# Streaming encoder step: norms transposed by token tile, first FFN products among the transpositions, wide sums handed over by tile

## What is computed

```python
xn = rmsnorm(x, g_mix);  proj = xn @ w_in            # first norm, then 9728 columns
h  = x + (gate_a * y_a + gate_b * y_b) @ w_out       # D x D
hn = rmsnorm(h, g_ffn)                               # second norm
gate, up = split(hn @ w_ffn_in)                      # 2 x 5632 columns
gate_c = causal_conv3(gate) + conv_b
h  = h + (silu(gate_c) * up) @ w_ffn_down            # 5632 x D
y  = rmsnorm(h, g_final)
```

## Time and profile before

| | |
|---|---|
| runs | 2498.18 us, median of 3 (2497.25 to 2504.71) |
| profiled execution | 2497.85 us by the same clock as the runs, span 2496.2 us |
| busy share of the span | PE 97 %, PEld 89 %, DVE 44 %, ACT 35 %, POOL 4 % |
| PE waits over 1 us | 15.9 us at the start for parameters, 7.9 us before the second norm's transpositions, some shorter |
| mean granted clock of PE | 0.989 of full |

### The profile page before, as it was taken

How to read it: one execution, slowest core, us unless ns; L and a number is a source line. 1 busy time by engine, 2 the same in 40 slices (tenths; PEclk the granted TensorE clock), 3 DMA queues, 4 the chain that set the end, 5 groups by cost and what they waited for, 6 DMA issues and landing times.

```text
span 2496.2 us, 44147 instructions
## 1 busy us (share of the span) xinstructions
PE 2431.5 (97%) x17372; PEld 2232.2 (89%) x17372; DVE 1104.6 (44%) x1743; ACT 870.8 (35%) x1311; POOL 108.6 (4%) x182
## 2 busy tenths in 40 slices
PE   6999999999899999999998999999999999999997
PEld 6888888888899999999877999999878999999886
DVE  4555656654433322344333544444233444444234
ACT  4444344443323322344223433333222333333232
POOL 4000000000010100000000000000000000000010
PEclk9999999999999999999999999999999999999999
DMA  5323222222533433344533344444333444444433
GB/s 167 105 74 81 78 77 74 74 72 71 132 119 94 124 98 92 96 127 125 169 124 109 112 126 126 126 126 124 127 126 118 132 126 126 126 127 141 128 129 127
DMA packets 414538, 284.14 MB, mean 114 GB/s; under 512 B 31728, under 2 KB 392690, under 8 KB 413536
## 3 DMA queue, kind: packets, MB, share of 16 engines
q1 hardware_dynamic: 405600, 259.16, 35.3%
q0 software_dynamic: 8832, 23.36, 3.4%
HBM read 275.55 MB, written 6.92 MB: 113 GB/s over the span
## 4 chain that ended last, share of the span: by engine, by line
PE 95%; DVE 2%; ACT 1%; DMA 1%; issue 1%; POOL 0%; DVEq 0%; SPq 0%; POOLq 0%; ACTq 0%
PE banks L1453 20%; PE banks L903 19%; PE banks L907 18%; PE banks L904 18%; PE banks L324 2%; PE banks L916 2%; PE banks L918 2%; PE banks L917 2%; PE banks L392 1%; PE banks L1316 1%; PE banks L472 1%; PE banks L1319 1%; PE banks L457 1%; PE banks L1414 1%; PE banks L485 0%
## 5 line engine op out<-in xcount | busy, mean ns | idle before, releaser
L893 DVE TENSOR_TENSOR w_lo<-w_raw,w_hi 128x1024 fp32r<-128x1024 f32 x482 | 590.1, 1225 | 964.5 <-ACT w_hi L888 964.2
L903 PE MATMUL banks<-x_hi,w_hi 128*128 128x384 f32 x2640 | 918.6, 348 | 8.3 <-DVE w_lo L893 8.3
L907 PE MATMUL banks<-x_hi,w_lo 128*128 128x384 f32 x2640 | 886.9, 336 | 0.0
L904 PE MATMUL banks<-x_lo,w_hi 128*128 128x384 f32 x2640 | 885.7, 335 | 0.0
L888 ACT ACTIVATE w_hi<-w_raw 128x1024 fp32r<-128x1024 f32 x482 | 511.3, 1061 | 1039.9 <-PE banks L907 595.5
L903 PEld LDWEIGHTS banks<-x_hi,w_hi 128*128 128x128 f32 x2640 | 497.6, 188 | 35.6 <-issue 11.9
L904 PEld LDWEIGHTS banks<-x_lo,w_hi 128*128 128x128 f32 x2640 | 498.5, 189 | 5.0 <-issue 0.3
L907 PEld LDWEIGHTS banks<-x_hi,w_lo 128*128 128x128 f32 x2640 | 497.6, 188 | 1.2 <-issue 1.2
L1453 PE MATMUL banks<-w_hi,act_hi 128*128 128x512 f32 x528 | 164.2, 392 | 4.6 <-DVE h_rows L2009 2.4
L1453 PE MATMUL banks<-w_lo,act_hi 128*128 128x512 f32 x528 | 164.2, 392 | 0.0
L1453 PE MATMUL banks<-w_hi,act_lo 128*128 128x512 f32 x528 | 163.2, 390 | 0.0
(11 more groups left out here) (401 smaller groups left out, 2294.4 us busy)
## 6 DMA issues: line engine op xcount, KB each, us to landing
w_raw<-in_w_ffn_in SPq DMA_DIRECT2D x176, 512.0 KB, 4.0
w_raw<-in_w_in SPq DMA_DIRECT2D x144, 512.0 KB, 3.8
w_raw<-in_w_ffn_down SPq DMA_DIRECT2D x88, 512.0 KB, 3.6
w_raw<-in_w_out SPq DMA_DIRECT2D x32, 512.0 KB, 3.6
w_raw<-in_w_o_a SPq DMA_DIRECT2D x16, 512.0 KB, 4.0
w_raw<-in_w_o_b SPq DMA_DIRECT2D x16, 512.0 KB, 3.9
w_raw<-in_w_in SPq DMA_DIRECT2D x20, 256.0 KB, 3.8
w_ukv_head<-in_w_ukv POOLq DMA_DIRECT2D x8, 512.0 KB, 3.9
```

The source lines that it names most:

```text
L893: nc.vector.tensor_tensor(lo[:, s], raw[:, s], hi[:, s].bitcast(F32), ALU.subtract).then_inc(lo_done, 1)
L903: nc.tensor.matmul(out, hi[:, s, k, :], xh[:, kt, :], start=kt == 0, stop=False)
L904: nc.tensor.matmul(out, hi[:, s, k, :], xl[:, kt, :], start=False, stop=False)
L907: last = nc.tensor.matmul(out, lo[:, s, k, :], xh[:, kt, :], start=False, stop=kt == 15)
```

## The change

1. `pe_norm` turns the first six kts token tile by token tile, each as soon as that token tile is scaled, and returns `further` for the kts 6 to 15, which keep their old order. A bank's count (`norm_ps`) is given with the third token tile.
2. `act_norm` and `dve_norm` make the second weight block (`act_hi(..., 1)`, `dve_lo(..., 1)`) inside their loop: before kt 8 in the first norm, before kt 12 in the second. The places where they were made after the norm leave them out.
3. In the second norm PE does the first FFN tile's products among the transpositions: kt 0 to 2 after the transpositions of kt 6 to 8, kt 3 to 5 after those of 9 to 11, the rest after the last. The first tile pair is taken out of the loop.
4. In a wide pass the last kt's products of token tile 0 and of token tile 1 add one to a new semaphore `acc_tile`, and `add_acc` waits for that per tile.

```diff
-        def pe_norm(src, first, ready, taken):
-            for kt in range(KD):
-                bank = 2 + kt % 6
-                if kt == 0:
-                    nc.tensor.wait_ge(ready, 3)
-                if kt >= 6:
-                    nc.tensor.wait_ge(taken, first * KD + kt - 5)
-                for t in range(3):
-                    last = transpose(ps[:, bank, t * P:t * P + P], src[:, t, kt * P:kt * P + P])
-                last.then_inc(E("norm_ps"), 1)
+        def pe_norm(src, first, ready):
+            turn = lambda t, kt: transpose(ps[:, 2 + kt % 6, t * P:t * P + P], src[:, t, kt * P:kt * P + P])
+            for t in range(3):
+                nc.tensor.wait_ge(ready, t + 1)
+                for kt in range(6):
+                    last = turn(t, kt)
+                    if t == 2:
+                        last.then_inc(E("norm_ps"), 1)
+
+            def further(kts):
+                for kt in kts:
+                    nc.tensor.wait_ge(E("xt_lo"), first * KD + kt - 5)
+                    for t in range(3):
+                        last = turn(t, kt)
+                    last.then_inc(E("norm_ps"), 1)
+            return further
...
-        def act_norm(first, gcol):
+        def act_norm(first, gcol, second, at):
             for kt in range(KD):
+                if kt == at:
+                    act_hi(second, 1)
...
-        def dve_norm(first, gcol):
+        def dve_norm(first, gcol, second, at):
             for kt in range(KD):
+                if kt == at:
+                    dve_lo(second, 1)
...
-            pe_norm(xt, 0, E("x_scaled"), E("xt_lo"))
+            pe_norm(xt, 0, E("x_scaled"))(range(6, KD))
...
+                        if kt == kts - 1 and t < 2:
+                            last.then_inc(E("acc_tile"), 1)
                     last.then_inc(blk_used, 1)
...
-            pe_norm(hn, 1, E("h_scaled"), E("xt_lo"))
-            pe.wait_ge(E("xt_lo"), KD + 8)
+            further = pe_norm(hn, 1, E("h_scaled"))
+
+            def first_gate(kts):
+                for kt in kts:
+                    pe.wait_ge(E("xt_lo"), KD + kt + 1)
+                    pe_block(T_FFN, kt // 8, ps[:, 0, 0:NT], [kt % 8])
+            further(range(6, 9))
+            first_gate(range(0, 3))
+            further(range(9, 12))
+            first_gate(range(3, 6))
+            further(range(12, KD))
+            first_gate(range(6, KD))
+            for s in range(2):
+                pe_block(T_FFN + 1, s, ps[:, 1, 0:NT])
             for hf in range(2):
-                with pe.Fori(0, HJ) as j:
+                with pe.Fori(1 - hf, HJ) as j:
...
-                            if q == 0 and s == 1 and hf == 0:
-                                pe.wait_ge(E("xt_lo"), 2 * KD)
...
-            act_norm(0, 80)
+            act_norm(0, 80, T_LORA, 8)
...
-            act_norm(1, 96)
+            act_norm(1, 96, T_FFN, 12)
...
-            dve_norm(0, 80)
+            dve_norm(0, 80, T_LORA, 8)
...
                 dve.wait_ge(E("acc_taken"), OPEN + done)
-                dve.wait_ge(blk_used, need)
                 for t in range(3):
+                    if t < 2:
+                        dve.wait_ge(E("acc_tile"), done * 2 + (t + 1))
+                    else:
+                        dve.wait_ge(blk_used, need)
...
-            dve_norm(1, 96)
+            dve_norm(1, 96, T_FFN, 12)
```

More of the change, by code:

```diff
@@ L1524, in _ @@
             for t in range(4):
-                act_next(t)
+                act_next(t) if t else act_hi(1, 0)
                 if t == 0:
@@ L1762, in ffn_act @@
                 t, n = j * 2 + (hf * T_HALF + T_FFN), j + hf * HJ
-                act_hi(t, 1, t * 16 + 96)
+                if before or hf:
+                    act_hi(t, 1, t * 16 + 96)
                 if before:
@@ L1831, in _ @@
             for t in range(4):
-                dve_next(t)
+                dve_next(t) if t else dve_lo(1, 0)
                 if t == 0:
@@ L2041, in ffn_dve @@
                 tap = lambda q: cprm[:, q, n:n + 1] if isinstance(n, int) else cprm[:, q, bass.ds(n, 1)]
-                dve_lo(t, 1)
+                if before or hf:
+                    dve_lo(t, 1)
                 if before:
```

## The result

The changed kernel's first four runs had a median of 2482.08 us (2479.36 to 2483.69), beside 2500.39 for the four of the kernel before: ratio 0.9924, interval 0.9905 to 0.9944. Over the whole study the changed kernel ran 20 times unedited (2479.4 to 2490.0, mean 2484.6) and the kernel before 82 times (2491.7 to 2506.6, mean 2500.3). The difference of the means is 15.7 us, with some 1.5 us of uncertainty from their scatter, where the prediction's sum was 10.7. The profiled execution took 2481.56 us, with a span of 2479.9 (before: 2496.2).

The account below looks back on a forecast made before the run. PE was taken to bound the kernel, so only its waits, half clock and the end could be won. Terms 0.4 - 5.2 - 3.5 - 2.4 = minus 10.7 us gave a median of 2487.4 us, range 2484.0 to 2493.0.

Parts of the forecast that it names:

- Pass ends: Behind wide passes, sums per token tile end PE's waits for banks and a late `w_lo`: minus 5.2 us.
- Second norm: Earlier sums, turning by token tile and FFN products among transpositions shorten PE's wait: minus 3.5 us, bounds minus 4.5 and 0.
- the deduction for the clock: At the second norm the clock falls until about 1371, so some 1 us of PE's work takes twice as long.
- First norm: Turning by token tile delays `x_hi` and the first products: plus 0.4 us, bounds minus 1 and plus 2.
- a hand-over in "24.71 + 1.3 + 1.2 + some 0.4": At the first norm, some 0.4 us of hand-over delay before the products, which were to start at 27.6.
- The end: Behind the last pass, sums end 1.3 us after the last product instead of 3.7: minus 2.4 us.
- Sum: All four edited places together: 0.4 - 5.2 - 3.5 - 2.4 = minus 10.7 us.
- the base: Whole kernel: the profiled execution's 2497.85 us, 0.33 us below the median, from which the forecast subtracted.
- The rival of the attention's clock: 870 to 1003, sequences' attention: share at half clock rises from 0.18 to 0.46, costing 18.5 us, median 2506; chance 0.02.
- the half clock through the mixed stretch: At the second norm the clock returns only at about 1378; term shrinks to 0.4 us, median 2490.5; chance 0.16.
- a hand-over that does nothing: At pass ends a `w_lo` holds DVE; the 5.2 and 2.4 us go, median 2497; chance 0.05.
- a late rise at the first norm: At the first norm the clock rises one us or more later, costing 2 us: 2489; chance 0.09.

Follow-up runs that it names:

- e4: The changed kernel with the first FFN tile's products behind all transpositions of the second norm; 2483.99 us, ratio 0.9943.
- e5: The changed kernel with the first norm's transpositions kt by kt again, the second weight block kept inside the norm; 2485.16 us, ratio 0.9942.
- e8: The changed kernel with the edits of e5 and e6 and the first projection tile's products among the first norm's transpositions; 2474.40 us, ratio 0.9888.
- e9: The kernel before, unedited, run again for a second profile; 2501.52 us, ratio 0.9993.
- e1: The kernel before with part 4 of the change alone (`acc_tile`, sums per token tile); 2491.2 us, ratio 0.9965.
- e2: The changed kernel without part 4, so norms and first FFN products only; 2495.8 us, ratio 0.9981.
- e10: The kernel before, unedited, run again for a third profile; 2501.46 us, ratio 1.0001.
- e6: The changed kernel with the first two `w_ukv` loads held back until the seventh attention tile is taken; 2479.67 us, ratio 0.9905.
- e12: The kernel before with the first two `w_ukv` loads held back until the latent projections have taken one more block; 2490.59 us, ratio 0.9963.
- e14: The kernel before, unedited, run again for a fourth profile of 637 to 1222 us; 2502.72 us in one run.
- e3: The changed kernel with the first norm of the kernel before (kt by kt, second weight block behind the norm); 2484.72 us, ratio 0.9938.
- e15: The changed kernel, unedited, run again for one more profile; 2482.07 us in one run.

## Why the prediction was wrong

The direction, the mechanism and the places were right; the median lay 5.3 us under the forecast and 1.9 us under the range.

- **Pass ends, -5.2 forecast, -5.6 measured** (1.6 + 2.8 + 1.2). Right. The added semaphore steps cost nothing that a row shows.
- **Second norm, -3.5 forecast, -4.4 measured.** The value at full clock (4.4) was worked out to the tenth: the second tile at 19.7 us behind the pass. What failed is the deduction for the clock. It did fall, but rose at 1361.5, 7.7 us behind the end of the pass, where I had put it some 10 us behind. So it was back ahead of the products, and the 0.9 us deducted were some 0.2: the first `x_hi` came that much later behind the pass than in e4, which had no fall there, and from there on ACT and DVE set the pace of the transpositions.
- **First norm, +0.4 forecast, -0.1 measured.** `x_hi` began at 19.63 for 19.75 forecast; the products at 27.14 for 27.6. The 0.4 us for a hand-over in "24.71 + 1.3 + 1.2 + some 0.4" was not there. What the section missed is the other half: e5 and e8 show that this edit holds 1.3 us, and with products among the transpositions 3.0, both lost to the turn by token tile.
- **The end, -2.4 forecast, -2.5 measured.** Right.
- **Sum, -10.7 forecast, -12.6 at the edited places.** The terms that were off by 0.4, 0.9, 0.5 and 0.1 us all erred to one side. That alone gives 2485.5 us by the prediction's base, inside the range.
- **The step that failed** is the base, and with it the lower end: the sum held everything unedited at the time of one profiled execution, so its term for the unedited stretches was nothing, where the first pair of profiles shows -6.7 us from 637 to 1222, and the range allowed "0.6 for the runs' own scatter". The stretch from 637 to 1222 scatters by 6.5 us in five profiles of one program (578.6 to 585.1), through the landing at 637 and 20 to 34 us at half clock. That was to be seen in part: the three runs shown lay 7.5 us apart, and the prediction used this only against a rival. The rival of the attention's clock was priced for a loss alone ("If the share at half rose"); the same mechanism working downward, fewer falls, was left out, and it is what carried the first four runs to 2482.1 (23.9 us at half clock in the profiled one; granted clocks of 0.991 to 0.993, where the mean over all runs of the kernel before is 0.988). With the three runs' own half-width, 3.7 us, in place of 0.6 the range would have begun near 2481. Chance has its part in the miss: the changed kernel's first four runs have a mean of 2481.8 us, its other 16 one of 2485.3, and all 20 one of 2484.6, inside the range. Chance has a part on the other side too: the base of 2498.18 lies 2.1 us under the mean of the kernel before.

What happened to the rivals: the half clock through the mixed stretch did not come, nor a hand-over that does nothing, nor a late rise at the first norm. Against the rival of the slower attention: from 870 to 1003 the granted clock was 0.91 to 0.92 in all kernels, six or seven short falls.

**Open.** All 82 runs of the kernel before and all 20 of the changed one give 15.7 us, 3.1 more than the edited places, with 1.5 of uncertainty. Averaged over four profiles of the one and five of the other, the edited stretches give 13.5 us (0.9 more than at equal clock, through a fall at 32 us in one of the four, the longer half clock at the second norm and e9's last pass) and the stretch from 637 to 1222 gives 4.2. The 4.2 us are mostly clock: the four profiles of the kernel before all have 34.1 us at half clock there, the five of the changed one 20.5 to 34.1, on average 25.9. But neither course belongs to one program. e1 is the kernel before up to 1222 us and had 27.3 us at half clock behind a full wait of 3.3; e2 and e4 are the changed kernel up to there and had 34.1 each, as e5 had, which differs at the first norm alone. Counted by program up to 1222 us, five profiles against seven, the difference shrinks from 4.2 to 2.4 us. Whether the changed program takes the shorter course more often, and through what, is not settled.

The runs' granted clocks say the same of the scatter. Of the kernel before, 22 runs at a mean clock of 0.987 took 2501.8 us on average and three at 0.991 took 2493.8; of the changed kernel five at 0.989 took 2487.4 and eleven at 0.991 took 2483.0. So much of what one program's runs differ by goes with the time at half clock.

The 187.81 us of e9 between 2295 and the last matmul have no fall in them. They lie in the last pass: from its first product's start to its last one's the 396 products took 92.2 us, in e10 90.5. Each takes a little longer throughout (0.233 us against 0.229), at a granted clock of 1.00. Why is not known.

## What to carry to other kernels

Hand over sums and banks per tile instead of per pass wherever the next user wants one tile only: it cost no time here and gave 9.8 of some 16 us. Turning by token tile pays where the tiles arrive one after the other (at most 1.6 us at the second norm) and loses where all are there (1.3 us at the first); products among transpositions pay wherever the transpositions are paced by other engines. And take the scatter of the base into the range from the runs shown, even if every edited place can be worked out to the tenth: a program of 2.5 ms has unedited stretches that move more than the edits' errors.

## What the runs showed of the hardware that was not expected

- The same program with the same DMAs waits 1.1 or 3.0 to 3.4 us for one weight block at 637 us (once and four times in five profiles); two loads issued by POOL beside it are a cause, since without them the wait was gone in three profiles of three (e6, e8, e12). What makes the difference between 1.1 and 3 us with the loads in place is not known.
- The clock falls behind short waits only sometimes. Behind 2.2 us of waiting at 29 us it fell in e1 and e14, and not in the kernel before, e3, e9, e10 or e12. Behind 2.9 to 3.5 us at 637 it fell in ten profiles and stayed in two (e5 and e15). Behind 1.1 and 1.3 us, or none, it stayed.
- It also falls with PE busy throughout: in the sequences' attention six or seven times, 3.4 us each, in all 17 profiles between 870 and 1003 us.
- The clock came back with nothing but transpositions on PE ahead of it (1361.5 here, 1371.9 before). And the fall at the second norm, where PE feeds ACT and DVE and they set the pace, cost some 0.2 us where the same 3.4 us between products cost 1.3 to 1.6.
- The granted clock is not the whole pace: in e9's last pass 396 products ran 1.9 % slower than in e10's, at 1.00 in both.
